# Fourier mixing between the two small norms of the latent attention, and the first weights' high parts before the first root

## What is computed

```
pf, mq, mk, mv, mo, mg, cq, ckv, kr = split_proj(h @ w_in[l])
y_f = fourier_mix(pf)                      # 256 x 64 Fourier transform, real part
... mLSTM, both directions, from mq, mk, mv, mo, mg ...
q = (rmsnorm(cq, g_qn) @ w_uq)             # queries, width 256 -> 4 heads x 96
kv = (rmsnorm(ckv, g_kvn) @ w_ukv)         # keys and values, width 128 -> 4 heads x 160
... rotary embedding of q and kr, softmax attention ...
x = x + ga1 * (concat[y_f, y_m, y_a] @ w_out[l])
```

## Time and profile before

| | |
|---|---|
| time, three runs | 1637.81 us median (1633.72 to 1641.09) |
| the profiled execution | 1635.65 us |
| its span, first to last instruction | 1633.8 us |
| PE busy | 1563.7 us, 96% of the span, granted clock 0.992 of full speed on the mean |
| DVE busy | 1059.7 us, 65% |
| ACT busy | 762.2 us, 47% |
| transfers | 253.86 MB, 155 GB/s on the mean |

### The profile page before, as it was taken

The page is one execution under the profiler, slowest core; times in us unless marked ns, Lnnn a source line. Parts: engine busy times, 40 slices in busy tenths (PEclk is TensorE's granted clock), DMA queues, the critical chain, the costliest instruction groups (busy, mean ns, idle before and its releaser), DMA issues.

```text
span 1633.8 us, 27313 instructions
## 1 busy us (share of the span) xinstructions
PE 1563.7 (96%) x9969; PEld 1373.7 (84%) x9969; DVE 1059.7 (65%) x1794; ACT 762.2 (47%) x1309; POOL 99.5 (6%) x165
## 2 busy tenths in 40 slices
PE   7999989999999999999899999999999998999997
PEld 6998788899999997876677888888887885899997
DVE  5567487788888888724765655455557955765564
ACT  5544544444444455344653541244224455665562
POOL 0011000000000000000300100001000001100000
PEclk9999999999999999999999999999999999999999
DMA  7665154487777733330322654455442452146562
GB/s 265 216 225 183 58 178 158 130 289 245 242 245 244 256 105 116 104 90 14 65 104 64 207 191 143 141 193 185 162 154 73 139 130 39 58 159 191 176 191 90
DMA packets 71497, 253.86 MB, mean 155 GB/s; under 512 B 7888, under 2 KB 11120, under 8 KB 71168
## 3 DMA queue, kind: packets, MB, share of 16 engines
q1 hardware_dynamic: 54048, 189.43, 34.9%
q0 software_dynamic: 17376, 63.44, 13.3%
HBM read 251.73 MB, written 1.11 MB: 155 GB/s over the span
## 4 chain that ended last, share of the span: by engine, by line
PE 83%; DVE 10%; ACT 3%; issue 3%; DMA 1%; DVEq 0%; SPq 0%; ACTq 0%
PE pair L1087 82%; ACT wh L586 1%; DVE sq L2299 1%; DVE uv L1761 1%; DVE wl L1720 1%; DVE sq L1801 1%; DVE small L1793 1%; DVE spent L1853 1%; PE pair L1131 1%; DVE uh_f L1853 1%; PE pair L1266 1%; ACT sq L654 0%; DMA uh_f<-in_mods 0%; DMA table<-in_table 0%; DVE ul L1750 0%
## 5 line engine op out<-in xcount | busy, mean ns | idle before, releaser
L1087 PE MATMUL pair<-uh,wh 128*128 128x256 f32 (+3 forms) x1864 | 581.9, 312 | 16.5 <-DVE ul L1750 9.7
L1720 DVE TENSOR_TENSOR wl<-ring,wh 128x1024 fp32r<-128x1024 f32 x350 | 426.6, 1223 | 253.1 <-ACT wh L586 247.1
L1087 PE MATMUL pair<-ul,wh 128*128 128x256 f32 (+3 forms) x1864 | 576.2, 309 | 0.0
L1087 PE MATMUL pair<-uh,wl 128*128 128x256 f32 (+3 forms) x1864 | 576.0, 309 | 0.0
L586 ACT ACTIVATE wh<-ring 128x1024 fp32r<-128x1024 f32 x350 | 366.9, 1052 | 260.4 <-PE pair L1087 253.1
L1087 PEld LDWEIGHTS pair<-uh,wh 128*128 128x128 f32 (+1 forms) x1864 | 346.8, 186 | 45.4 <-issue 17.9
L1087 PEld LDWEIGHTS pair<-uh,wl 128*128 128x128 f32 (+1 forms) x1864 | 347.0, 186 | 23.7
L1087 PEld LDWEIGHTS pair<-ul,wh 128*128 128x128 f32 (+1 forms) x1864 | 346.9, 186 | 22.6
L1087 PE MATMUL pair<-hh,wh 128*128 128x512 f32 (+1 forms) x512 | 172.6, 337 | 0.8
L1087 PE MATMUL pair<-hl,wh 128*128 128x512 f32 (+1 forms) x512 | 172.0, 336 | 0.0
L1087 PE MATMUL pair<-hh,wl 128*128 128x512 f32 (+1 forms) x512 | 172.0, 336 | 0.0
(11 more groups left out here) (279 smaller groups left out, 1991.8 us busy)
## 6 DMA issues: line engine op xcount, KB each, us to landing
ring<-in_w_stream SPq DMA_DIRECT2D x350, 512.0 KB, 3.7
uh_f<-in_mods POOLq DMA_DIRECT2D x48, 512.0 KB, 6.1
mod_w<-in_mods POOLq DMA_DIRECT2D x48, 512.0 KB, 3.8
uv<-c_rows POOLq DMA_DIRECT2D x4, 512.0 KB, 7.1
ml<-ml_dram POOLq DMA_DIRECT2D x4, 512.0 KB, 8.3
table<-in_table SPq DMA_DIRECT2D x1, 1849.5 KB, 12.2
res<-in_x SPq DMA_DIRECT2D x4, 256.0 KB, 4.1
res<-in_mem SPq DMA_DIRECT2D x1, 1024.0 KB, 14.4
```

The lines of the kernel that those rows point to most:

```text
L1087: ins = pe.matmul(*operands, **flags)
L1720: tt(wl[:, s, :], ring[:, s, :], wh[:, s, :].bitcast(F32), ALU.subtract).then_inc(S("w_lo"), 1)
```

## The change

Three edits. At the start, ACT makes the high parts of pieces 0 to 2 ahead of the root of norm "mix" instead of behind it. In the latent attention the Fourier transforms move from behind the values to the two small norms, on PE and on ACT. In layer 0 the transform of the context stands between the norms of `cq` and `ckv`, and that of the latent tokens behind the norm of `ckv`; in layer 1 the stage "fa" stands between the two norms and "fy" behind the second. And the constant matmuls of "cq_0" and "ckv_0" go, 14 of 512 columns. The table of PSUM jobs is put into the new order.

```diff
 SPIN = {"mix": (0, 19, 6), "sb": (0, 6, 6), "xattn": (6, 8, 6), "ffn": (6, 8, 6),
-        "n2_0": (7, 17, 5), "n1_1": (18, 17, 6), "n2_1": (5, 8, 5),
-        "cq_0": (0, 4, 6), "ckv_0": (4, 6, 6)}
+        "n2_0": (7, 17, 5), "n1_1": (18, 17, 6), "n2_1": (5, 8, 5)}
...
-                                    ("ckv", 1, "act"), ("pf", 2, "act"), ("uq", 4, "act"), ("rot", 5, "dve"),
-                                    ("kn", 4, "act"), ("va", 4, "act"),
+                                    ("ckv", 1, "act"), ("pf", 2, "act"),
                                     ("fa0", 2, "act"), ("fy0", 2, "act"), ("fa1", 2 * (_w - 1), "act"), ("fy1", 2 * (_w - 1), "act"),
+                                    ("uq", 4, "act"), ("rot", 5, "dve"), ("kn", 4, "act"), ("va", 4, "act"),
...
             act.wait_ge(S("early_in"), 16)
+            split(2)
             root("mix", P, T, D)
-            split(2)
             round_tiles("mix", LAT)
...
+                def spectrum(s, phase):
+                    sc = slice(cols.start + s * T, cols.start + (s + 1) * T)
+                    for ft in range(2):
+                        b = full(act, f"{phase}{s}_{l}", ft)
+                        if phase == "fa":
+                            last = act.activation(fa[:, ft, :, :], b[:, :].rearrange("p (a t) -> p a t", a=2), ACT.Copy)
+                        else:
+                            last = act.activation(yf[:, ft, sc], b[:, 0:T], ACT.Copy)
+                        emptied(last, "act")
                 root(f"cq_{l}", P, n, 256)
                 square(f"ckv_{l}", 0, ckv[:, :], P, 512)
-                root(f"ckv_{l}", P, 512, 128)
+                spectrum(0, "fa")
+                if l:
+                    root(f"ckv_{l}", P, 512, 128)
+                spectrum(0, "fy")
+                if l == 0:
+                    root(f"ckv_{l}", P, 512, 128)
+                    spectrum(1, "fa")
+                    spectrum(1, "fy")
...
                 norm(f"cq_{l}", P, n)
-                norm_ckv = f"ckv_{l}"
+                spectrum(0, "fa")
+                if l == 0:
+                    spectrum(0, "fy")
                 pe.wait_ge(S("norm_rstd"), NORM[f"cq_{l}"] + 1)
-                norm(norm_ckv, P, 512)
+                norm(f"ckv_{l}", P, 512)
+                if l == 0:
+                    spectrum(1, "fa")
+                    spectrum(1, "fy")
+                else:
+                    spectrum(0, "fy")
...
```

More of the change, by code:

```diff
@@ L938, in _ @@
                     emptied(act.activation(va[:, j, :], b[:, 0:384], ACT.Copy), "act")
[L939 to L947, removed]
                 units = range(UNIT0["mctx0"], UNIT0["mlat1"]) if l == 0 else range(UNIT0["mlat1"], len(UNITS))
@@ L1527, in _, with spectrum @@
                     last.then_inc(S("gcol_full"), 1)
+                cn = tab("cn").rearrange("p (b n) -> p b n", b=2)
+                sn = tab("sn").rearrange("p (b n) -> p b n", b=2)
+                def spectrum(s, phase):
+                    c0 = cols.start + s * T
+                    for ft in range(2):
+                        b = claim(f"{phase}{s}_{l}", ft)
+                        wait_emptied(pe, f"pf_{l}" if phase == "fa" else f"fa{s}_{l}", ft)
+                        for nb in range(TB):
+                            if phase == "fa":
+                                last = mm(b[:, nb * T:(nb + 1) * T], pf[:, ft, c0 + nb * P:c0 + (nb + 1) * P],
+                                          tab("cdsd"), start=True, stop=True)
+                            else:
+                                mm(b[:, 0:T], fa[:, ft, nb, 0:P], cn[:, nb, :], start=(nb == 0), stop=False)
+                                last = mm(b[:, 0:T], fa[:, ft, nb, P:2 * P], sn[:, nb, :], start=False, stop=(nb == 1))
+                        finish(last)
                 norm(f"cq_{l}", P, n)
-                norm_ckv = f"ckv_{l}"
+                spectrum(0, "fa")
+                if l == 0:
+                    spectrum(0, "fy")
                 pe.wait_ge(S("norm_rstd"), NORM[f"cq_{l}"] + 1)
-                norm(norm_ckv, P, 512)
+                norm(f"ckv_{l}", P, 512)
+                if l == 0:
+                    spectrum(1, "fa")
+                    spectrum(1, "fy")
+                else:
+                    spectrum(0, "fy")
                 pe.wait_ge(S("norm_out"), normed(f"cq_{l}")[1])
@@ L1556, in _ @@
                     finish(mm(b[:, 0:384], ckv[:, j * P:(j + 1) * P], ukv[:, 256:640], start=True, stop=True))
[L1558 to L1575, removed]
                 pe.wait_ge(S("mla_keys"), l + 1)
```

## The result

| | before | after |
|---|---|---|
| time, median | 1637.76 us (9 runs) | 1626.27 us (9 runs, 1624.40 to 1632.50) |
| the profiled execution | 1635.65 us | 1625.92 us |
| its span | 1633.8 us | 1624.1 us |

The ratio is 0.9934, with a 95% interval of 0.9917 to 0.9950: 10.8 us less, 8.2 to 13.6. The forecast was 1628.0, a saving of 9.6 to 9.8 us.

What follows compares the result with a forecast made beforehand. The prediction took PE's products to bound the kernel. Savings of 4.1 (start), 1.85 (layer 0) and 3.65 (layer 1) sum to 9.6 us, from the median 1637.81 to 1628.2, forecast as 1628 us, range 1621 to 1635.

Steps and rivals of the forecast that it cites:

- PE sets the pace, and every part is passed on whole: Whole kernel: products on PE set the pace, so a saving at any of the three places moves all that follows equally.
- The start: First products: copies ahead of the root bring DVE's first `uv` 3.1 us earlier and PE starts without a gap; 4.1 us saved.
- The term of 2.7: Start: PE's first product begins at 16.7 us, right behind the constant matmuls, saving 2.7 us.
- The clock's 1.4 us: Start: without the gap PE keeps full clock, so 16 matmuls take 1.9 us instead of 3.3, saving 1.4 us.
- one of the prediction's own signs of being wrong: Start and both layers' small norms: a low granted clock at any of these three places would show the prediction wrong.
- The term of 1.85: Layer 0 latent attention: scores start at 753.4 instead of 755.24 us, gaining 1.85; ceiling 4.4, floor +0.25 to -1.15.
- the prediction's floor: Layer 1 small norms: with the clock as low as before, 3.0 us less gain, leaving 0.65 us.
- the 3.65: Layer 1 latent attention: scores start at 1357.1 instead of 1360.76 us, a gain of 3.65 us.
- The clock falls in the new gap of layer 0: Layer 0 norms: PE's 1.2 us idle lowers the clock, shrinking the gain by 1.6 to 3.0 us, to 1630 to 1631; chance 0.17.
- The start gives nothing: Start: first products still meet a late `ul` or low clock; 5.5 us saving remains, 1632.3 us; chance 0.12.
- The later pieces hold PE up: Fifth piece at the start: a late landing makes PE wait 1 to 2 us, giving 1629.5 to 1630 us; chance 0.07.
- Slower through the low clock in all of layer 0: Layer 0 latent attention: without constant matmuls the clock stays low up to the scores, 18 us slower, 1656 us; chance 0.04.

Runs made afterwards that it cites:

- layer 0 alone: Kernel before with only layer 0's transforms moved between its small norms and its 14 constant matmuls removed; ratio 0.9980 (0.9969 to 0.9992).
- the kernel with the gap bridged: Kernel before with 30 instead of 19 constant matmuls behind the sums of the first root, filling PE's gap at the start; ratio 0.9996 (0.9983 to 1.0008).
- the start alone: Kernel before with only the three copies put ahead of the first root, both layers in the old order; ratio 0.9972 (0.9958 to 0.9985).
- layer 1 alone: Kernel before with only layer 1's "fa" moved between the small norms and "fy" behind the second; ratio 0.9980 (0.9965 to 0.9995).

## Why the prediction was right

**PE sets the pace, and every part is passed on whole.** Right: PE is busy for 96% of the span after as before, and the three parts made alone add up to the whole (11.2 and 10.8 us), as far as their intervals tell.

**The start.** Right in its steps: three copies ahead of the root, the first `uv` 6.04 us behind the sums (forecast 14.5 less the 8.47 at which the sums stood before, 6.03), PE's first product without a gap. The constant matmuls took 5.55 us and not 5.12, so the first product came 8.58 us behind the sums, not 8.2; the first `ul` had ended 0.94 us before it, where 0.4 was forecast to spare. The term of 2.7 is 2.3 in the trace after and 2.6 to 3.2 in three others. The clock's 1.4 us rest on less. The 16 in the earlier trace rows counts weight loads; the row has 15 matmuls, which makes the term 1.5. In the traces with the old order a low stretch follows the gap in six of seven (it doesn't in that of layer 0 alone, with 1.71 us idle), in the six with the new order never. Its price is not resolved by the kernel with the gap bridged.

**Layer 0.** The order of events was right: from the first "fa" to the queries 12.84 us, forecast 13.3, from there to the scores 17.72, forecast 17.7, and the scores wait for the last copy of the values. What the schedule didn't have is the low clock at the sums: from them to the first "fa" it is 3.13 us instead of 1.42, so the stretch in this trace is only 0.59 us shorter than before. A low clock at one of the three places was one of the prediction's own signs of being wrong, and here it came. The term of 1.85 still came out at 3.3 (1.3 to 5.1), within its bounds, with some luck. It was worked out from a trace in which layer 0 stood at full clock throughout; with the run of tiny products in its place, only two of thirteen traces do (the kernel before and the start alone, both 34.28 us). With the low clock the old order takes 35.20 to 36.19 us, the new one 32.98 to 33.69, about 2.5 less: the old order mostly pays the low clock too, which the prediction couldn't know from its trace.

**Layer 1.** Right in size: 21.45 us from the sums to the scores, forecast 21.6. The reason given for it was incomplete. The low clock was put down to the gap of 1.62 us; the runs show that it can begin behind the tiny products without the gap, and that the gap prolongs it. In the old order the clock was low in all seven traces that have the run in that place, in the new one in one of five. Why it mostly stays up in the new order isn't shown: in layer 0 full products follow the run at once as well, and there the clock fell in all five traces. So a part of this term came out for a reason that the prediction didn't have, which is luck. The one low trace (layer 1 alone, 23.00 us) is the case of the prediction's floor, but with a low stretch of 3.4 us instead of 6: 2.2 us were left of the 3.65, not 0.65.

**The rivals.** *The clock falls in the new gap of layer 0:* it falls in that stretch in every trace of the new order that has the run, but ahead of the gaps (0.47 and 0.29 us), and the old order pays it too, in six of eight traces; so the gain does not shrink. *The start gives nothing:* refuted by the start alone. *The later pieces hold PE up:* no. The fifth piece was issued at 13.40 and took 9.8 us to land, where before it was issued at 15.62 and took 8.3. The row of the kernel after, of that load:

```profile
ring<-in_w_stream SPq DMA_DIRECT2D x1, 512.0 KB, 9.8
```

It landed at 23.2 against 23.9, and the sums, too, began 0.75 us earlier in this execution, so the earlier issue bought nothing: the trace agrees with the rule of the Trainium skill that the prediction named (DMA: Bandwidth & Descriptors, "Queues, rings and completion order"). In all fourteen traces this piece landed 15.4 to 15.8 us behind the start of the sums, though it was issued from 5.6 to 7.2 us behind it. It cost nothing either, since ACT's copy at 24.46 was released by PE, 1.3 us after the landing.

*Slower through the low clock in all of layer 0:* no; the low stretch there is some 3.4 us long in the kernel after (0.52 over a window of 3.5).

## What to carry to other kernels

Where PE sets the pace, look for what it waits for in each small norm, and put work there that doesn't depend on the norm; constant matmuls that stood in such a wait should then go, since here they cost some 3.6 us. A stretch read from one execution may stand at either clock: compare it in several before sizing a gain by it. A run of tiny products is cheap by its own row and may be paid for behind it, so read the granted clock behind such runs and not only behind gaps; spreading them has a price of its own.

## What was not expected of the hardware

The granted clock fell at the end of, or behind, 3.31 us of 32 tiny products that the profile shows as busy, with no gap, in 11 of 13 traces in layer 0; moved in layer 1, the run took the fall along, and a gap of 1.62 us without it was followed by 1.00. Gaps with no such run ahead of them went before a fall too: at the start those of 1.97 to 2.84 us in six of six traces, the one of 1.71 us not. The Trainium skill (TensorE: Matmul & The Clock Gate, "HAM oscillation") ties such falls to idle gaps of the engine; the falls at the start are of that kind, and those behind the tiny products of layer 0, with no gap, are not. Two points stay open: why the new order escapes the fall in layer 1 in four of five traces but in layer 0 in none, and what sets the other low stretches, which stand in different places from one execution to the next (221 to 224, 303 to 306 and 590 to 593 us in the trace after, 159 to 166, 224 to 227 and 801 to 804 in the next one of the same kernel).
